# First attention's lead-in and its fillers, placed elsewhere in the hand-written order of steps of a fused 3-layer block

## The reference, cut to what matters

```python
def shared_kv(h, positions, kv_norm_w, kv_w, k_norm_w):
    u = rms_norm(h, kv_norm_w)
    k, v = jnp.split(u @ kv_w, 2, axis=-1)
    ...
    k = rope(rms_norm(k, k_norm_w), positions)
    return k, v

def swa_layer(h, k, v, positions, norm_w, in_w, q_norm_w, sinks, out_w):
    u = rms_norm(h, norm_w)
    q, gate = jnp.split(u @ in_w, 2, axis=-1)
    q = rope(rms_norm(q.reshape(b, s, ATT_HEADS, HEAD_DIM), q_norm_w), positions)
    o = swa_sink_attention(q, k, v, sinks)
    return (o * jax.nn.silu(gate)) @ out_w
```

## Time and profile before

| | before |
|---|---|
| median of 3 runs | 1384.82 us (1384.52 to 1387.69) |
| the profiled execution's own time | 1384.84 us |
| its span in the trace | 1382.0 us |
| mean granted TensorE clock | 0.996 of full |
| TensorE busy | 1349.0 us, 98% of the span |
| VectorE, ScalarE, GpSimd busy | 60%, 49%, 37% |
| DMA, mean | 85 GB/s |

### The profile page before, as it was taken

How to read it: one execution, slowest core, us unless ns; L and a number is a source line. 1 busy time by engine, 2 the same in 40 slices (tenths; PEclk the granted TensorE clock), 3 DMA queues, 4 the chain that set the end, 5 groups by cost and what they waited for, 6 DMA issues and landing times.

```text
span 1382.0 us, 17831 instructions
## 1 busy us (share of the span) xinstructions
PE 1349.0 (98%) x6632; PEld 1062.8 (77%) x6632; DVE 824.7 (60%) x1415; ACT 677.8 (49%) x1131; POOL 517.9 (37%) x257
## 2 busy tenths in 40 slices
PE   9989999999999999999999999999998999999997
PEld 6867777777778878757888887676677888888786
DVE  6775564757567744685676413376755645544666
ACT  7654635636366543685565312355545332322463
POOL 3552553635230034456100434116433655555200
PEclk9999999999999999999999999999999999999999
DMA  5321312212232223211333233030012332333331
GB/s 196 92 70 53 92 62 92 77 62 76 77 92 92 92 92 92 61 47 47 92 102 116 87 126 118 31 122 3 23 54 77 101 98 92 103 96 92 122 107 61
DMA packets 33804, 116.94 MB, mean 85 GB/s; under 512 B 4144, under 2 KB 4656, under 8 KB 33464
## 3 DMA queue, kind: packets, MB, share of 16 engines
q1 hardware_dynamic: 32408, 111.62, 25.9%
q10 hardware_dynamic: 1312, 4.20, 0.9%
HBM read 113.71 MB, written 2.10 MB: 84 GB/s over the span
## 4 chain that ended last, share of the span: by engine, by line
PE 89%; DVE 5%; ACT 2%; issue 2%; DMA 1%; POOL 1%; ACTq 0%; DVEq 0%
PE bank L1310 85%; PE bank L1774 1%; PE bank L1608 1%; DMA h<-in_xT 1%; ACT wsh L864 0%; DVE arena L1969 0%; POOL arena L773 0%; DVE arena L2049 0%; DMA ring<-in_wstream 0%; DVE parts1l L1884 0%; PE bank L1484 0%; PE bank L1519 0%; DVE wsl L1855 0%; DVE arena L2341 0%; DVE ssacc L1850 0%
## 5 line engine op out<-in xcount | busy, mean ns | idle before, releaser
L710 POOL TENSOR_TENSOR wsl<-ring,wsh 128x1024 fp32r<-128x1024 f32 x141 | 343.5, 2437 | 535.9 <-ACT wsh L864 535.8
L864 ACT ACTIVATE wsh<-ring 128x1024 fp32r<-128x1024 f32 x196 | 207.2, 1058 | 456.2 <-PE bank L1310 432.7
L1310 PE MATMUL bank<-parts1h,wsh 128*128 128x512 f32 (+1 forms) x736 | 292.8, 398 | 6.9 <-POOL wsl L710 2.2
L1310 PE MATMUL bank<-parts1h,wsl 128*128 128x512 f32 (+1 forms) x736 | 285.8, 388 | 0.0
L1310 PE MATMUL bank<-parts1l,wsh 128*128 128x512 f32 (+1 forms) x736 | 285.7, 388 | 0.0
L1310 PE MATMUL bank<-parts0h,wsh 128*128 128x512 f32 x696 | 277.9, 399 | 4.0 <-issue 1.3
L1310 PE MATMUL bank<-parts0h,wsl 128*128 128x512 f32 x696 | 271.4, 390 | 0.0
L1310 PE MATMUL bank<-parts0l,wsh 128*128 128x512 f32 x696 | 271.0, 389 | 0.0
L1310 PEld LDWEIGHTS bank<-parts1h,wsh 128*128 128x128 f32 x736 | 138.5, 188 | 43.8 <-issue 9.0
L1310 PEld LDWEIGHTS bank<-parts1l,wsh 128*128 128x128 f32 x736 | 138.8, 189 | 28.9 <-issue 2.2
L1310 PEld LDWEIGHTS bank<-parts0h,wsh 128*128 128x128 f32 x696 | 130.7, 188 | 39.4 <-issue 9.8
(11 more groups left out here) (325 smaller groups left out, 1792.5 us busy)
## 6 DMA issues: line engine op xcount, KB each, us to landing
ring<-in_wstream SPq DMA_DIRECT2D x204, 512.0 KB, 3.6
arena<-in_alibi ACTq DMA_DIRECT2D x2, 1024.0 KB, 5.5
outT<-arena SPq DMA_DIRECT2D x8, 256.0 KB, 2.8
h<-in_xT SPq DMA_DIRECT2D x4, 256.0 KB, 6.7
h<-in_xT ACTq DMA_DIRECT2D x4, 256.0 KB, 7.4
ring<-in_wstream SPq DMA_DIRECT2D x2, 256.0 KB, 4.7
arena<-in_frow ACTq DMA_DIRECT2D x1, 512.0 KB, 3.4
arena<-in_cmpb ACTq DMA_DIRECT2D x1, 496.0 KB
```

What stands on the lines that cost most here:

```text
L710: return nc.gpsimd.tensor_tensor(dst, src, hi.bitcast(F32), ALU.subtract)
L864: nc.scalar.activation(wsh[n % NSET][:, :], src, ACT.Copy).then_inc(*done("high", ("high", L)))
L1310: return nc.tensor.matmul(*args, **kw)
```

## The change

The order of five steps is changed, nothing else: no instruction is added, removed or resized.

```diff
-    out += [("kv", 0), ("norm", 2), ("kv", 1), ("nb", 2), ("hn", "attn"), ("kv", 2), ("kv", 3)]
+    out += [("kv", 0), ("norm", 2), ("kv", 1), ("nb", 2), ("hn", "attn", 0), ("kv", 2), ("hn", "attn", 1), ("kv", 3)]
...
-    out += [("qn", 1), ("gate", 2)] + ro[1] + [("gate", 3), ("kT",)] + [("q", 1, b) for b in range(4)]
+    out += [("qn", 1), ("gate", 2)] + ro[1] + [("gate", 3)] + [("q", 1, b) for b in range(4)] + [("kT",)]
...
-    out += [("gate", 6)] + swa[:7] + [("gate", 7), ("qT", 1), ("psp", 1)]
-    between = {u: [("pp", 1, m)] for m, u in enumerate((1, 2, 8, 9))} | {10 + m: [("ao", 0, m)] for m in range(6)}
+    out += [("gate", 6)] + swa[:7] + [("gate", 7)]
+    between = {0: [("qT", 1)]} | {u: [("pp", 1, m)] for m, u in enumerate((2, 4, 6, 9))} | {10 + m: [("ao", 0, m)] for m in range(6)}
...
-    out += body[:k] + [("half",)] + body[k:]
+    out += body[:k] + [("half",), ("psp", 1)] + body[k:]
```

## The result

The changed kernel took 1397.98 us (median of 5 runs, 1392.72 to 1398.38), the kernel before 1386.96 us (5 runs, 1384.52 to 1388.94) in the same comparison: a ratio of 1.0082 with an interval of [1.0066, 1.0098], so slower by 11.0 us. The sign is as forecast; the forecast time, 1391.3 us, is 6.7 us too low, and its range ended at 1394.5. The profiled execution took 1398.38 us with a span of 1395.5 us, 13.5 us more than before's 1382.0, at a mean granted clock of 0.988 in place of 0.996.

The account below looks back on a forecast made before the run. TensorE, busy 1349.0 of 1382.0 us, was taken as the bound nearly everywhere. From 1384.84 us, +0.7 (rows in halves), +4.6 (key transposes), -0.5 (attention's order) and +1.7 (clock) gave 1391.3 us; range 1387.4 to 1394.5.

Parts of the forecast that it names:

- Part one: Normalized rows in two halves: the wait before gate 0 goes, some 2.0 us come before gate 1; +0.7 us.
- Part two: Key transposes behind q 1: its 1.02 us wait goes, 5.6 us come before gate 4; +4.6 us.
- The turn of the banks: gate 4 opens the bank of q 1's first job, so it waits 5.6 us for DVE's first multiply.
- Part three: The attention's order behind gate 7: first aV's wait goes, waits of 0.8 and 2.1 us come; -0.5 us taken.
- the sum: Whole kernel: 1384.84 + 0.7 + 4.6 - 0.5 + 1.7 = 1391.3 us.
- The clock: Behind gate 4's 5.6 us wait the granted clock falls to half once; +1.7 us.
- the earlier trace: Profile of before: behind a 2.21 us wait from 1068.3 the clock fell to half, 1.7 us lost; used as the price.
- The rival of the second fall: Another clock fall, behind gate 7 until pp 0 or at gate 1's wait: 1.7 us each, 1393.0 to 1395; chance 0.13.
- The rule for the fall: At gate 4: half clock is the default and recent activity releases it, so a fall after the wait is near certain.

Follow-up runs that it names:

- The repeat: The changed kernel run again without any edit, against the kernel before: 1395.93 us, ratio 1.0065.
- before with 24 matmuls more late: Kernel before plus 24 matmuls of 128x512 in the third layer's sparse attention, against the kernel before: 1387.51 us, ratio 1.0013.
- halves with POOL: Kernel before with the normalized rows in two halves and POOL making low parts from gate 1's block on: 1385.35 us, ratio 0.9992.
- halves with DVE: Kernel before with only the normalized rows in two halves, DVE still making gate 1's low part: 1389.57 us, ratio 1.0020.

## Why the prediction was wrong, by its own steps

**Part one** held. No wait before `gate 0`, 2.27 before `gate 1` (forecast some 2.0), +1.0 in place of +0.7. The chain was right in kind and size: within the stage gate 1's copy slipped by 0.96 us, forecast 0.89. That DVE's queue was the cause is shown by the kernel in which POOL takes gate 1's block.

**Part two** held in every row: no wait before `q 1`, 5.57 us before `gate 4` (forecast 5.6, bounds 5.2 to 6.0), released by L2209. The turn of the banks is shown as the cause by two kernels.

**Part three** had its waits right in kind and place: the first `aV`'s gone, 0.72 at the second (forecast 0.8), 2.81 at `pp 0` (forecast 2.1). The size was off: DVE's split of the embedding input took 1.97 us, where the forecast took 1.23 from the row of another step. The waits sum to 3.97 us, against 3.85 before, and in the kernel with this part alone the stage grew by 0.5; the -0.5 of the sum was too hopeful by 0.6 to 1.0.

**The clock** is the step that failed: "I take one such fall behind the 5.6 us wait, **+1.7**; none would be 0, and a second one behind the 2.0 us wait of part one another 1.7 (one chance in three, left out of the sum)." The one fall stood for 6.8 us at half clock where that of the earlier trace rows stood for 3.4, and cost 2.1. A second came, for 1.7, not before `gate 1`, where it was set at one in three, but behind `pp 0`'s 2.81 us. Over all profiles such falls are as likely as not: 4 of 7 with the wait before `gate 1` have one, and 5 of 7 with that before `pp 0`. By these counts two waits of this length are worth some 2.2 us together (an estimate, 1.7 times 4/7 and 5/7), and the sum had nothing for them. The rival of the second fall had the mechanism and named the place, with 1393.0 to 1395 us and a chance of 0.13.

So in the stage the forecast has 6.5 us and the trace 9.5: 0.3 in part one, 0.6 in part three (by its waits, +0.1 in place of -0.5), 0.4 for the first fall and 1.7 for the second make the 3.0. Over the runs the difference is 11.0 us. The 1.5 us beyond the stage agree with a longer fall in the sparse attention: over the runs the loss to the clock rose by 6.8 us, of which the stage's two falls, 10.2 us at half clock, are 5.1. The forecast had no such term. The repeat (1395.93 against 1385.89 us), whose stage alone is longer by 10.9 in its profile, doesn't need it, so that its size, and whether the change has a part in it, stays open. Of the 6.7 us between forecast and median the last 2.1 are the base: before's median was 1386.96 in this comparison, and the sum was made against one execution that, with a clock of 0.996, had lost 5.5 us to the clock where 9.4 is the mean. The median of 3 runs, which it met to 0.02 us, didn't show that.

**The rule for the fall.** The Trainium skill, TensorE: Matmul & The Clock Gate, "What's actually happening", has half clock as the default, from which activity frees TensorE, so that a fall follows a long wait. With the wait of 5.57 us filled by matmuls the window stays at 1.00, and in all five profiles that have it unfilled the clock falls, so the runs agree. The same page of the Trainium skill, "Part 4: PE-mode transpose", has transposes as not counting as activity in the same way, and the forecast gave this little weight. The runs don't settle it. The windows from 582 to 611 us of before, with transposes throughout, ran at 1.00, but the same stretch in before with 24 matmuls more late had a fall behind the same 1.61 us wait. And in the sparse attention, where 52 of the 157 matmuls are transposes, the clock fell without a wait; no run tells these from the other small matmuls there.

## What to carry to other kernels

Where an ordered list also hands out the banks, moving a step by a few places gives all its neighbours other banks: write down, for the first jobs behind the old and the new place, whose reader each now waits for. Here that alone was 5.57 us, and two steps further on it was nothing. Taking away a wait pays only if the chain behind the next block, which was just in time, is not delayed by it; halves with POOL saved 1.6 us in the stage, halves with DVE lost 1.0. And a clock's falls are to be priced from several profiles and the spread over runs, not from one profile: the gain of a shorter stage (2.8 us) vanished in a loss of 2.6 us elsewhere. With the sparse stage filled the time fell by a further 5.0 us; what the filling gives in the order of before is open.

## What the runs showed of the hardware

TensorE's granted clock fell to half (1.2 of 2.4 GHz) with no wait at all: in all 18 profiles between 922 and 960 us, where most of its matmuls are small or transposes, for 3.4 to 20.5 us. How long differs between executions of one program (27.7 and 33.7 us for the same 157 matmuls). In the profiles without added matmuls there, the lengths stand in four bunches: 27.5 to 27.8 us in six, 30.3 in two, 33.7 to 33.8 in four, 35.1 in three. Single runs of before lose from 5.5 to about 15 us to the clock, and these falls are likely, but not shown, to be most of that. Twelve further matmuls of 128x512 there, whose results nobody reads, went with a mean loss of 5.3 in place of 12.0 us. What sets the length of the fall is not settled: a delay of 0.9 us went with a long one, one of 5.5 us with a short one, and only means over several runs tell anything.

Nor does the length of a wait decide alone whether a fall follows. These are the stage's waits of over 1.2 us that several kernels share, and three outside it, over all 18 profiles; a fall counts when it begins in the wait or within 2 us behind it:

| wait of TensorE | profiles with it | with a fall |
|---|---|---|
| 5.57 us, `gate 4` | 5 | 5 |
| 2.81 us, `pp 0` | 7 | 5 |
| 2.27 us, `gate 1` | 7 | 4 |
| 2.21 us, | 18 | 11 |
| 1.96 us, at 81 us | 18 | 10 |
| 1.61 us, first `aV` | 10 | 1 |
| 1.5 us, 22 us ahead of the earlier trace rows's | 18 | 0 |
| 1.31 us, `gate 0` | 7 | 0 |

Two waits of 1.34 and 1.37 us, one 2 us behind the other in a single kernel, had one fall between them. All but the fall at `gate 4`, with 6.8 us at half clock, are 3.4 us long. The changed kernel is one of the seven without a fall behind the 2.21 us of the earlier trace rows: its wait ends at 1086.47, and the clock around it is 1.00:

```profile
1084.00:1088.00 4.00, 1.79 (x9) 1.30 (x8) 3.01 (x4) 2.28 (x3) 4.00 (x3) 1.00 0.19 33
```

These seven are just the profiles whose fall in the sparse attention lasted 17.1 or 20.5 us; in the eleven where it lasted up to 10.2 us, the fall of the earlier trace rows came too. So the falls of one execution hang together, though the runs don't show by what.
